# A two-block transformer kernel in float32: the three passes of every product run over their columns in descending order

## The reference

```python
def first_block(x, ...):                       # 512 tokens, DEPTH = 2 layers
    for l in range(DEPTH):
        mod = c_act @ w_ada[l] + b_ada[l]
        u = h @ w_in[l] + b_in[l]              # 1024 -> 3 latents, q, k, v, two gates
        q = rms_norm(q_lat, g_q_lat[l]) @ w_uq[l]
        kv = rms_norm(kv_lat, g_kv_lat[l]) @ w_ukv[l]
        merged = sigmoid(gate_mla) * (y_mla @ w_branch_mla[l]) + sigmoid(gate_sb) * (y_sb @ w_branch_sb[l])
        x = x + gt1 * (merged @ w_out[l])
        up = causal_depthwise_conv(h @ w_up[l], w_conv[l], b_conv[l])     # 1024 -> 2 * 2816
        x = x + gt2 * ((silu(a) * v_ff) @ w_down[l])                      # 2816 -> 1024
def second_block(x, ctx, ...):                 # 512 tokens and 256 context tokens
    # layer 0: u = h @ w_pw1; gate; depthwise conv of 31 taps; layer norm; silu; @ w_pw2, for x and ctx
    # layer 1: q, k, v = h @ wq, h @ wk, h @ wv; attention of 16 heads over 768 keys; @ wo
    # both:    x = x + gate * rmsnorm((silu(h @ w1) * (h @ w3)) @ w2)
```

## Time and profile before

| | |
|---|---|
| median of 3 runs | 3287.12 us (3286.65 to 3288.83) |
| profiled execution, span from first to last instruction | 3282.0 us |
| median less that span | 5.1 us |
| TensorE matmuls, busy | 3152.4 us, 96% of the span |
| VectorE, ScalarE, GpSimd, busy | 1570.4, 1186.3, 815.1 us |
| granted TensorE clock, mean | 0.987 of full |
| matmuls of lines 435, 436, 437 | 4016 each |

### The profile page before, as it was taken

One profiled execution on the slowest core, in us unless ns is written; L12 is line 12 of the kernel. 1 busy time (PEld: TensorE's weight loads), 2 busy tenths in 40 slices (PEclk: granted clock), 3 DMA queues, 4 the chain that ended last, 5 costly groups with the idle time before them and its releaser, 6 DMA issues.

```text
span 3282.0 us, 38620 instructions
## 1 busy us (share of the span) xinstructions
PE 3152.4 (96%) x15546; PEld 2472.2 (75%) x15546; DVE 1570.4 (48%) x2204; ACT 1186.3 (36%) x1764; POOL 815.1 (25%) x399
## 2 busy tenths in 40 slices
PE   6999999999999999999989899999999979999998
PEld 4657778887665777778867477888888658878887
DVE  3572146464375124334378644322334899653234
ACT  3443244243444224424321244111112558632223
POOL 4302445555320343444401000000000039500000
PEclk9999999999999999999999999999999999999999
DMA  6413436665430555453335211222221110122332
GB/s 237 129 42 110 147 91 200 217 192 164 128 113 7 180 175 171 144 178 93 98 81 130 53 49 55 65 65 65 61 62 58 39 39 1 39 70 88 106 89 79
DMA packets 429892, 337.21 MB, mean 103 GB/s; under 512 B 16637, under 2 KB 411223, under 8 KB 417428
## 3 DMA queue, kind: packets, MB, share of 16 engines
q1 hardware_dynamic: 428272, 334.23, 33.5%
q0 software_dynamic: 1248, 0.46, 0.1%
q10 hardware_dynamic: 196, 0.07, 0.0%
HBM read 319.58 MB, written 2.10 MB: 98 GB/s over the span
## 4 chain that ended last, share of the span: by engine, by line
PE 58%; DVE 5%; POOL 4%; ACT 1%; issue 1%; SPq 0%; DMA 0%; POOLq 0%; DVEq 0%; ACTq 0%
PE PS L435 17%; PE PS L436 17%; PE PS L437 17%; POOL p L2579 4%; PE PS L524 1%; PE PS L831 1%; PE PS L592 1%; PE PS L637 1%; DVE both_tmp L1371 0%; DVE q_parts L1693 0%; PE PS L1026 0%; DVE Wl L1274 0%; PE PS L536 0%; DVE stat_t L1347 0%; SPq L2621 0%
## 5 line engine op out<-in xcount | busy, mean ns | idle before, releaser
L435 PE MATMUL PS<-Hh,Wh 128*128 128x512 f32 x2208 | 875.4, 396 | 20.5 <-DVE both_tmp L1371 8.3
L2534 POOL TENSOR_TENSOR Wl<-raw,Wh 128x1024 fp32r<-128x1024 f32 (+2 forms) x254 | 618.0, 2441 | 986.6 <-ACT Wh L2045 986.6
L436 PE MATMUL PS<-Hl,Wh 128*128 128x512 f32 x2208 | 861.8, 390 | 0.0
L437 PE MATMUL PS<-Hh,Wl 128*128 128x512 f32 x2208 | 861.4, 390 | 0.0
L2045 ACT ACTIVATE Wh<-raw 128x1024 fp32r<-128x1024 f32 (+2 forms) x442 | 436.1, 988 | 400.4 <-PE PS L437 349.5
L435 PEld LDWEIGHTS PS<-Hh,Wh 128*128 128x128 f32 x2208 | 416.1, 188 | 127.9 <-issue 62.6
L437 PEld LDWEIGHTS PS<-Hh,Wl 128*128 128x128 f32 x2208 | 415.8, 188 | 88.0
L436 PEld LDWEIGHTS PS<-Hl,Wh 128*128 128x128 f32 x2208 | 416.4, 189 | 67.6 <-issue 3.4
L1274 DVE TENSOR_TENSOR Wl<-raw,Wh 128x1024 fp32r<-128x1024 f32 (+3 forms) x188 | 217.6, 1157 | 389.6 <-ACT Wh L2045 389.3
L1952 DVE SCALAR_TENSOR_TENSOR cv<-PS,vcols,cv 128x510 f32<-128x510 f32 (+1 forms) x176 | 123.7, 744 | 216.8 <-ACT cv L2456 216.8
L435 PE MATMUL PS<-g_h,Wh 128*128 128x512 f32 x528 | 206.7, 391 | 3.5 <-POOL Wl L2534 3.5
(11 more groups left out here) (383 smaller groups left out, 4759.3 us busy)
## 6 DMA issues: line engine op xcount, KB each, us to landing
raw<-in_ffn_w SPq DMA_DIRECT2D x108, 512.0 KB, 3.6
mod_w<-in_w_mod SPq DMA_DIRECT2D x48, 1024.0 KB, 5.0
raw<-in_w_up SPq DMA_DIRECT2D x88, 512.0 KB, 4.6
mod_w<-in_w_ada SPq DMA_DIRECT2D x40, 1024.0 KB, 4.9
raw<-in_w_in SPq DMA_DIRECT2D x62, 512.0 KB, 4.0
UQ<-U SPq DMA_DIRECT2D x128, 99.4 KB, 2.2
raw<-in_w_down SPq DMA_DIRECT2D x32, 384.0 KB, 5.0
raw<-in_conv_w_pw SPq DMA_DIRECT2D x24, 512.0 KB, 4.1
```

Source lines behind the costliest of these rows:

```text
L435: pe.matmul(o, wh, xh, start=start, stop=False, skip_group_check=True)
L436: pe.matmul(o, wh, xl, start=False, stop=False, skip_group_check=True)
L437: return pe.matmul(o, wl, xh, start=False, stop=stop, skip_group_check=True)
L2534: pool.tensor_tensor(low, src, high.bitcast(F32), ALU.subtract).then_inc(*mark("w_low_pool", one[0]))
```

## The change

In `three`, the output columns and both moving tiles are replaced by views that run from the last column to the first. Column 511 of the moving tile is read first and its result is written to column 511 of the bank first; column 0 comes last. The stationary tiles are as before. The sums are the same ones in the same places, in the same order of passes and of input channels; nothing is added, removed or moved on any engine, and every other line of the program only has its number raised by one. In the built program the moving operand and the output of these matmuls start at their last element and have a step of -1.

```diff
         def three(o, wh, wl, xh, xl, start, stop):
 
+            o, xh, xl = o[:, ::-1], xh[:, ::-1], xl[:, ::-1]
             pe.matmul(o, wh, xh, start=start, stop=False, skip_group_check=True)
             pe.matmul(o, wh, xl, start=False, stop=False, skip_group_check=True)
             return pe.matmul(o, wl, xh, start=False, stop=stop, skip_group_check=True)
```

## The result

| | before | after |
|---|---|---|
| median | 3287.97 us (4 runs, 3286.65 to 3289.26) | 3345.22 us (4 runs, 3337.22 to 3346.34) |
| ratio | | 1.0169, 95% interval 1.0154 to 1.0183 |
| span of the profiled execution | 3282.0 us | 3344.5 us |

What follows compares the result with a forecast made beforehand. TensorE's matmul pace was taken to bound the kernel. All costs of the change summed to 0, so 3282.0 us of span and 5.1 us around it gave 3287.1 us, range 3254 to 3444 us.

Steps and rivals of the forecast that it cites:

- What bounds the kernel: Whole kernel: TensorE's matmuls fill 96% of the span, so a changed matmul's pace goes into the time one for one.
- The 5.1 us that the sum took around the span: Outside the profiled execution: 5.1 us added to the 3282.0 us span to reach 3287.1 us.
- hand-overs, writes and the accumulation cost nothing: Changed matmuls: same semaphores, bank and operand bytes, and a column still revisited after 512 columns; cost 0.
- I take the end at no cost: Changed matmuls: of prices from no cost to 2172 us for a step of -1, 0 was chosen; chance 0.50.
- the one with broken rows: Latent values: moving rows read in four pieces still start every 226.7 ns, so an address jump at every 128th column is free.
- The argument from pairs: Changed matmuls: descending columns stay in the same aligned pairs, so a stage handling pairs finds the same pair; cost 0.
- a few nanoseconds more per matmul: Changed matmuls: a dearer turn at each row's end, 33 us by operand place, 157 us at most; chance 0.20.
- The spread of 2.7 ns: Groups of six: 1.050 us on gb_h and gb_l against 1.034 on Hh and context, 2.7 ns more a matmul.
- The rival at half pace: Changed matmuls: a slow stage pairs columns only in ascending order, 2172 us more, 5459 us in all; chance 0.17.
- The test by lengths: Matmuls of 512 and 256 columns: equal change in nanoseconds means a cost per matmul, twice means per column.
- The unchanged lines: Lines 913 to 915, 1104 and 1135 should keep their pace in every case; otherwise the cause is not the step.

Runs made afterwards that it cites:

- write_only: Against the changed kernel: only the bank is written from the last column to the first, moving rows read in ascending order; 3287.33 us, ratio 1.0001.

## Why the prediction was wrong, point by point

**What bounds the kernel** was right. Pace went into time nearly one for one: the changed matmuls took 56.8 us more, and at the same granted clock of 0.987 the span grew by 53.4. The chain still names the three lines at 17% each, and the waits swallowed little: the largest group is 15.6 us where it was 17.6. The 5.1 us that the sum took around the span hold 1.8 us outside it; the rest was the spread between executions, and as the sum was set to the median it did not move the forecast.

```profile
PE PS L525 <- DVE stat_v L1345: 15.6, 8, 6.1
```

**That hand-overs, writes and the accumulation cost nothing** was right, and `write_only` shows it by itself. The rule weighed there, of the Trainium skill's "PSUM — Partial Sum Buffer", section "Specifications (TRN2)", that a non-contiguous pattern slows matmuls, does not reach a descending write: ratio 1.0001.

**The step that failed** is "I take the end at no cost. The row nearest to the change is the one with broken rows". The term put at 0 for reading with a step of -1 measured 6.4 ns on each of 9264 matmuls of 512 columns. Those rows break at every 128th column, 512 bytes. Blocks of 64 columns (256 bytes) and halves show that walks of this kind are free, and blocks of 16 and of 4 that walks broken more finely are not. The row was the nearest in kind, and it varied the pattern at a scale where nothing happens. It bounded the cost of a jump and said nothing of many small ones. Why the small ones cost is not known.

**The argument from pairs** ("two neighbouring columns stay neighbours") excluded too little. Blocks of 4 keep four neighbours, 16 bytes, in ascending order and lose as much. "SBUF — State Buffer" of the Trainium skill, section "Specifications (TRN2)", gives lines of 16 bytes, wants two hits on each for full bandwidth and puts a penalty on each cross to a new line. All the walks here have four hits to a line and cross 127 times in a row of 512 columns, so by that rule they should pace alike. They do not, 226.9 against 233.3 ns, and the measurement decides.

**The rival "a few nanoseconds more per matmul"** is the case that came, and the range of 3254 to 3444 us held the time only through its upper bound. Its mechanism, a dearer turn at the row's end, is wrong: descending halves begin elsewhere and pay the same, ascending halves begin elsewhere and pay nothing. So that the range held is luck. Its size was bracketed: 33 us by the spread between the earlier trace rows, 157 us at most, measured 57. Its count was off: it charged 12048 matmuls alike, but the 1728 of 256 columns on the context paid 0.2 ns, and 9264 paid 6.4 ns. The spread of 2.7 ns was a bad measure as well. It averaged 16 ns over six matmuls, but all of it was on the three long ones: `gb_h` had 232.0 ns at 512 columns before the change and 117.8 at 256. So the trace before already held 5 ns on a long row, behind the 16 ns between the earlier trace rows.

**The rival at half pace** fell. Its hint, that the excess over the columns exists at 2.4 GHz only the earlier trace rows, pointed the right way: the loss too exists at 2.4 GHz only. (The stretch of the earlier trace rows is not the one stretch at 1.2 GHz; the trace has 15 of them, 84 us together.) As a bound of 2172 us it was far too wide.

**The test by lengths** ("by the same nanoseconds ... per matmul; if by twice, per column") left out the third answer, which came: next to nothing on the short rows and 6.4 ns on the long ones.

**The unchanged lines** kept their pace, as said.

## What to carry to other kernels

Read moving rows of float32r in ascending order, or at least in ascending blocks of 256 bytes, if the rows are longer than 256 columns and TensorE sets the time; a write to PSUM from the last column to the first was free here. A trace row bounds an unseen pattern only at its own scale: ask at which distance in bytes the row breaks and at which the change does. And where TensorE is full for 96% of the span, six nanoseconds on nine thousand matmuls are 1.7%, so a "no cost" needs a row that is good to a nanosecond.

## What the runs showed of the hardware that I had not expected

- A descending read costs 6.4 ns on 512 columns, 3.5 on 384, between -1.1 and 1.7 on 256, and nothing at 1.2 GHz. On 512 columns the 6.4 ns are against an undisturbed ascending stream; beside 256-column rows without the 64-byte offset it was 2.7 ns, and in the kernel with narrow passes -1.1. It costs the same for steps of one column and for blocks of 4 and 16 columns (up to 64 bytes), and nothing for blocks of 64 (256 bytes) and 256; 32 was not run.
- Descending writes to PSUM are free, with accumulation as well.
- Changing the weight load can slow a matmul of the same columns: with half the weight columns in one pass of three the ascending pace went from 226.9 to 229.8 ns, and with a load from a single column to 230.6 ns, though less was read. The time went from 3288 to 3310 us and from 3289 to 3316.
- A narrow second and third pass cost 5 ns a group more than the distances in even streams add up to, and the 5 ns are on the wide pass beside them, 231.9 ns for 226.9.
